# A decode step with sparse attention on one core: fewer transfers for the sample queries and masks, and the last four output tiles in two passes over the tokens

## The reference, cut to what matters

```python
# 512 prompt tokens and 8 x 4 sample tokens, D_MODEL 2048, 8 heads x 128
q, k, v, ga, qi, ki, wi, u, gb = _project(x, pos, w_in)        # one input projection
# attention: an indexer scores all causal keys, each query keeps the best k
scores = _index_scores(qi, wi, ki_all)          # samples: 1024 cached + 4 new keys
_, idx = lax.top_k(scores, topk)
s = einsum(q, k_sel) * HEAD_DIM ** -0.5         # samples read paged keys and values
o = softmax(s) @ v_sel
# pooling mixer p: trailing means over 2/4/8/16 tokens, then a 256 x 256 map per group
mixed = concat([a * silu(ga), p * silu(gb)])
h = DEEPNORM_ALPHA * x + einsum('btc,cd->btd', mixed, w_out)
mu, var = mean(h, -1), mean((h - mu) ** 2, -1)
y = (h - mu) * rsqrt(var + LN_EPS) * ln_g + ln_b
```

## Time and profile before

| what | value |
|---|---|
| median of 3 runs | 1173.95 us (1172.24 to 1175.3) |
| the profiled execution's own time | 1169.77 us |
| its span, first to last instruction | 1168.0 us |
| busy, share of the span | PE 96%, PEld 90%, DVE 54%, ACT 27%, POOL 30% |
| mean granted TensorE clock | 0.985 |
| chain that ended last, by engine | PE 82%, DVE 7%, SP's queue 4%, issue 3%, DMA 3% |

### The profile page before, as it was taken

How to read it: one execution, slowest core, us unless ns; L and a number is a source line. 1 busy time by engine, 2 the same in 40 slices (tenths; PEclk the granted TensorE clock), 3 DMA queues, 4 the chain that set the end, 5 groups by cost and what they waited for, 6 DMA issues and landing times.

```text
span 1168.0 us, 29727 instructions
## 1 busy us (share of the span) xinstructions
PE 1126.3 (96%) x11836; PEld 1048.8 (90%) x11836; DVE 636.5 (54%) x1173; ACT 318.4 (27%) x593; POOL 354.4 (30%) x150
## 2 busy tenths in 40 slices
PE   6999999999999999999997889999999999999995
PEld 5888889999999999999997888888889889999992
DVE  3566667896547557562364574655546443232236
ACT  4333334223332322332231221211212332122111
POOL 2323222333334334333330313221322233443410
PEclk9999999999999999999999999999999999999996
DMA  8542242233333333335414799788878785233103
GB/s 259 135 113 78 64 113 69 80 92 94 83 83 82 83 92 95 88 98 157 118 28 105 245 327 296 259 302 271 302 254 295 231 281 143 73 89 90 54 0 153
DMA packets 202157, 171.56 MB, mean 147 GB/s; under 512 B 22802, under 2 KB 182986, under 8 KB 200818
## 3 DMA queue, kind: packets, MB, share of 16 engines
q1 hardware_dynamic: 188666, 161.40, 44.8%
q10 hardware_dynamic: 13376, 8.53, 2.4%
HBM read 159.57 MB, written 9.90 MB: 145 GB/s over the span
## 4 chain that ended last, share of the span: by engine, by line
PE 82%; DVE 7%; SPq 4%; issue 3%; DMA 3%; ACT 1%; DVEq 0%; ACTq 0%
PE acc L1126 66%; PE acc L1490 2%; PE bank L1184 2%; PE bank L1427 2%; PE acc L1543 2%; PE bank L1301 1%; DVE scoreP L1753 1%; PE bank L1320 1%; DVE top L1749 1%; PE acc L1454 1%; SPq L455 1%; DMA xnat<-in_x_prompt 1%; SPq L561 1%; SPq L458 1%; DVE win L1994 1%
## 5 line engine op out<-in xcount | busy, mean ns | idle before, releaser
L653 POOL TENSOR_TENSOR wL<-rawW,wH 128x1024 fp32r<-128x1024 f32 (+1 forms) x146 | 354.2, 2427 | 766.5 <-ACT wH L675 766.5
L1126 PE MATMUL acc<-actH,wH 128*128 128x272 f32 (+1 forms) x2304 | 493.6, 296 | 1.2 <-DVE actL L1667 1.2
L1126 PE MATMUL acc<-actH,wL 128*128 128x272 f32 (+1 forms) x2304 | 477.6, 289 | 0.0
L1126 PE MATMUL acc<-actL,wH 128*128 128x272 f32 (+1 forms) x2304 | 476.4, 288 | 0.0
L1126 PEld LDWEIGHTS acc<-actH,wH 128*128 128x128 f32 (+1 forms) x2304 | 361.6, 189 | 31.5 <-issue 29.8
L1126 PEld LDWEIGHTS acc<-actL,wH 128*128 128x128 f32 (+1 forms) x2304 | 362.8, 189 | 0.0
L1126 PEld LDWEIGHTS acc<-actH,wL 128*128 128x128 f32 (+1 forms) x2304 | 360.3, 189 | 0.0
L675 ACT ACTIVATE wH<-rawW 128x1024 fp32r<-128x1024 f32 (+1 forms) x146 | 153.2, 1053 | 272.2 <-PE acc L1126 241.2
L2098 DVE SCALAR_TENSOR_TENSOR y<-y,bank 128x512 f32 (+1 forms) x16 | 11.0, 688 | 123.5 <-PE bank L1607 121.5
L1705 DVE SCALAR_TENSOR_TENSOR scoreP<-relu,wiN,scoreP 128x256 f32<-128x256 f32 (+2 forms) x54 | 45.4, 881 | 33.4 <-ACT relu L732 33.4
L1858 DVE STREAM_TRANSPOSE kPage<-kPage 128x1024 f32<-128x1024 f32 x30 | 37.2, 1239 | 46.5 <-DMA kPage<-in_cache_k 45.6
(11 more groups left out here) (210 smaller groups left out, 928.3 us busy)
## 6 DMA issues: line engine op xcount, KB each, us to landing
rawW<-in_w_in SPq DMA_DIRECT2D x112, 512.0 KB, 3.9
vPage<-in_cache_v SPq DMA_DIRECT2D x64, 512.0 KB, 7.0
kPage<-in_cache_k SPq DMA_DIRECT2D x60, 512.0 KB, 5.0
rawW<-in_w_out SPq DMA_DIRECT2D x32, 512.0 KB, 3.9
y<-in_x_prompt SPq DMA_DIRECT2D x4, 1024.0 KB, 8.0
out_y_prompt<-y SPq DMA_DIRECT2D x8, 512.0 KB, 2.8
xnat<-in_x_prompt SPq DMA_DIRECT2D x2, 1024.0 KB, 7.7
xnat<-in_x_prompt ACTq DMA_DIRECT2D x2, 1024.0 KB, 11.3
```

Of the source, the lines that this page charges most:

```text
L653: pool.tensor_tensor(wL[:, slot, :, 0:width], rawW[:, slot, :, 0:width], wH[:, slot, :, 0:width].bitcast(F32), ALU.subtract).then_inc(stag ...
L1126: last = pe.matmul(acc[t.slot][0:width, e, 0:HT], w[:, u.slot, k, 0:width], a[:, kk, e * HT:(e + 1) * HT], start=(half == 0 and k == 0 and ...
```

## The change

Three parts.

- **Queries.** `qS` is stored once to DRAM (`qD`), SP waits for that store, and four transfers, one for each strip of 32 partitions, read it back, instead of 16.
- **Masks.** DVE writes the table straight in the order that the mask wants (`dropS`, in the tile `U`, which is not in use yet), in two `tensor_scalar` and a memset; eight transfers of whole rows store it; and each mask is one transfer whose source is repeated for the four quarters, here and in the groups. ACT and DVE wait for the stores before they write `U`.
- **Output.** The first twelve tiles stay. The last four are multiplied for tokens 0 to 255 first, then their weights are loaded and split again and they are multiplied for tokens 256 to 543 (`out_part`: 24 matmuls with each half of a weight tile). The statistics, shift, correction and last pass of tokens 0 to 255 stand between the late parts.

```diff
+TWICE = 4
+WHOLE = KC - TWICE
+EARLY_T = 2 * P
...
-                for j in range(QUARTERS):
-                    stand_alone(sp)
-                    sp.dma_start(probS[SPAN * j:SPAN * (j + 1), :],
-                                 dropD.rearrange("s a r c -> (s a) r c")[:, ds(at, NT), :]).then_inc(mask_in[x % 2], 16)
+                stand_alone(sp)
+                sp.dma_start(probS[:], dropD.rearrange("b s a t c -> b (s a t) c")[ds(at, 1), :, :]
+                             .to_broadcast([QUARTERS, SPAN, LP])).then_inc(mask_in[x % 2], 16)
...
+            sp.dma_start(qD.rearrange("j s n -> (j s) n"), qS[:].rearrange("p h n -> p (h n)")).then_inc(q_out, 16)
+            sp.wait_ge(q_out, 16)
             for side in range(SIDES):
-                for j in range(SIDES):
-                    sp.dma_start(qAll[STREAK * side:STREAK * (side + 1), j, :],
-                                 qS[STREAK * j:STREAK * (j + 1), :, :].rearrange("p h n -> p (h n)")).then_inc(q_spread, 16)
+                sp.dma_start(qAll[STREAK * side:STREAK * (side + 1), :, :], qD.rearrange("j s n -> s j n")).then_inc(q_spread, 16)
...
             for side in range(SIDES):
                 for a in range(HALF):
-                    sp.dma_start(dropD[side, a, :, 0:HP].rearrange("r (p n) -> r p n", p=PAGES),
-                                 scoreS[:, 0:PAST].rearrange("r (p s n) -> r p s n", p=PAGES, s=SIDES)[:, :, side, :]
-                                 ).then_inc(drop_out, 16)
-            for a in range(HALF):
-                sp.dma_start(dropD[0, a, :, HP:LP], scoreS[:, PAST:L]).then_inc(drop_out, 16)
-            sp.dma_start(dropD[1:SIDES, :, :, HP:LP].rearrange("s a r c -> r (s a) c"),
-                         outside[0:NS, 0:NS].unsqueeze(1).to_broadcast([NS, (SIDES - 1) * HALF, NS])).then_inc(drop_out, 16)
+                    sp.dma_start(dropD[:, side, a, :, :], dropS[:, side, :]).then_inc(drop_out, 16)
...
+            for j in range(TWICE):
+                load_tile(wo_view, (WHOLE + j) * P, TILE_D + KC + j)
...
+            def out_part(tile, half):
+                t, u = tile_turn(tile), turn(2 * tile + half, 4)
+                e, cols = (0, slice(0, EARLY_T)) if tile < TILE_D + KC else (1, slice(EARLY_T, T))
+                pe.wait_ge(stage_ready[u.slot], u.read)
+                if half == 0:
+                    pe.wait_ge(acc_copied[t.slot], t.free)
+                for k in range(HU):
+                    for w, parts in ((wH, (actH, actL)), (wL, (actH,))):
+                        for a in parts:
+                            last = pe.matmul(acc[t.slot][:, e, 0:cols.stop - cols.start], w[:, u.slot, k, :],
+                                             a[:, (1 - half) * HU + k, cols], start=(half == 0 and k == 0 and w is wH and a is actH),
+                                             stop=(half == 1 and k == HU - 1 and w is wL))
+                last.then_inc(tile_ready[t.slot] if half else stage_free[u.slot // 2], 1)
...
+            for n in range(WHOLE + 1, KC + 2):
+                out_part(TILE_D + n, 0)
+                part_rows(n - 1)
+                out_part(TILE_D + n, 1)
             shift_turned("t0", (0, 1), 2)
+            out_part(TILE_D + KC + 2, 0)
+            part_rows(KC + 1)
             pe.wait_ge(gb_in, 16 * 8)
+            shift_back("t0")
+            correction(0, (0, 1))
+            out_part(TILE_D + KC + 2, 1)
+            correction(0, (2, 3))
+            out_part(TILE_D + KC + 3, 0)
+            part_rows(KC + 2)
+            correction(1, (0, 1))
+            out_part(TILE_D + KC + 3, 1)
+            correction(1, (2, 3))
+            part_rows(KC + 3)
             shift_turned("t1", (2, 3, 4), 4)
...
-                    own.step(dve.memset(outside[0:NS, 0:NS], MASKED))
-                    own.wait()
-                    dve.tensor_scalar(scoreS[:], scoreS[:], PICKED / 1.5, MASKED, ALU.is_gt, ALU.mult).then_inc(drop_ready, 1)
+                    dve.memset(dropS[:, 1:SIDES, HP:LP], MASKED)
+                    dve.tensor_scalar(dropS[:, 0, HP:LP], scoreS[:, PAST:L], PICKED / 1.5, MASKED, ALU.is_gt, ALU.mult)
+                    dve.tensor_scalar(dropS[:, :, 0:HP].rearrange("r s (p n) -> r s p n", p=PAGES),
+                                      scoreS[:, 0:PAST].rearrange("r (p s n) -> r p s n", p=PAGES, s=SIDES),
+                                      PICKED / 1.5, MASKED, ALU.is_gt, ALU.mult).then_inc(drop_ready, 1)
```

More of the change, by code:

```diff
@@ L1616, in _, with part_rows @@
                     unit(TILE_D + j + 1, 1, i, 2)
-            unit(TILE_D + KC - 1, 0)
-            rows(0, 7)
-            unit(TILE_D + KC - 1, 1)
-            rows(1, 7)
+            unit(TILE_D + WHOLE - 1, 0)
+            rows(0, 5)
+            unit(TILE_D + WHOLE - 1, 1)
+            def part_rows(n):
+                copied(TILE_D + n)
+                j, late = n % 2, n >= KC
+                b = tb(f"{'ab'[late]}{n - (KC if late else WHOLE)}")
+                dst = take(b)
+                for at in range(2):
+                    t = at + 2 * late
+                    last = pe.transpose(dst[:, at * P:(at + 1) * P], raw[:, j, t * P:(t + 1) * P], ident)
+                if late:
+                    last = pe.transpose(dst[0:NS, 2 * P:3 * P], raw[:, j, NP_:T], ident)
+                full(b, last)
             def shift_turned(name, tiles, ready):
@@ L1641, in _ @@
             pe.wait_ge(gb_in, 16 * 8)
-            b = tb("t0")
-            pe.wait_ge(bank_free[b.slot], b.read)
-            correction(0)
-            shift_turned("t1", (2, 3, 4), 4)
-            b = tb("t1")
-            pe.wait_ge(bank_free[b.slot], b.read)
-            for n in (2, 3):
-                take(tb(f"t{n}"))
-            for t in range(1, TT + 1):
+            shift_back("t0")
+            correction(0, (0, 1))
+            out_part(TILE_D + KC + 2, 1)
+            correction(0, (2, 3))
@@ L2124, in _, with part_added, part_gained @@
                     gained(2 * i + j)
-                own.leave(KC // 2 - 1)
+                own.leave(WHOLE // 2)
             own.step(dve.memset(mv[:], 1.0))
-            for j in range(2):
-                residual(KC - 2 + j, j, KC // 2 - 1)
-                statistics(KC - 2 + j)
-                if j == 0:
-                    gained(KC - 2)
+            def part_added(n):
+                late = n >= KC
+                d = n - TWICE if late else n
+                cols = slice(d * P, (d + 1) * P)
+                lo = 2 * late
+                b = tb(f"{'ab'[late]}{n - (KC if late else WHOLE)}")
+                src = bank_wait(dve, b)
+                if late:
+                    at = y[0:NS, TT, cols]
+                    own.step(dve.scalar_tensor_tensor(at, at, ALPHA, src[0:NS, 2 * P:3 * P], ALU.mult, ALU.add))
+                at = y[:, lo:lo + 2, cols]
+                dve.scalar_tensor_tensor(at, at, ALPHA, src[:, 0:2 * P].rearrange("p (t c) -> p t c", t=2),
+                                         ALU.mult, ALU.add).then_inc(bank_free[b.slot], 1)
+                own.wait()
+                dve.wait_ge(bank_free[b.slot], b.read)
+                for t in range(lo, TT + 1 if late else 2):
+                    m = P if t < TT else NS
+                    own.step(dve.bn_stats(bn[0:m, t, d, :], y[0:m, t, cols]))
+                own.wait()
+            def part_gained(n):
+                late = n >= KC
+                d = n - TWICE if late else n
+                cols = slice(d * P, (d + 1) * P)
+                lo = 2 * late
+                own.step(dve.tensor_tensor(y[:, lo:lo + 2, cols], y[:, lo:lo + 2, cols],
+                                           gbc[:, cols].unsqueeze(1).to_broadcast([P, 2, P]), ALU.mult))
+                if late:
+                    own.step(dve.tensor_tensor(y[0:NS, TT, cols], y[0:NS, TT, cols], gbc[0:NS, cols], ALU.mult))
             def aggregate(tiles):
```

138 lines of the change are left out of this document (97 added, 41 removed).

## The result

The changed kernel takes 1158.89 us (median of 6 runs, 1156.77 to 1160.58), the kernel before 1172.12 us (median of 6, 1167.22 to 1175.30): ratio 0.9886, 95% interval 0.9865 to 0.9906. So it is 13.2 us faster. The forecast was 1162.0 us, in a range from 1155 to 1169, on the right side and 3.1 us too high. Of these 3.1 us, 1.8 are the kernel before, whose median was 1173.95 us in three runs and is 1172.12 us in six; of the gain itself 11.9 us were forecast and 13.2 us came.

What follows compares the result with a forecast made beforehand. Bound: the order in SP's queue at the start of the page transfers, PE itself behind it, and the tail. 9.1 us (queries, masks) + 2.8 us (output) = 11.9 us off 1173.95 gave 1162.0 us, range 1155 to 1169.

Steps and rivals of the forecast that it cites:

- SP passes the first mask 9.9 us earlier: SP's queue ahead of the first mask's end: queries save 3.8 us, table 3.7, the mask's issue 2.4.
- The waits for the mask and the key pages go: PE in the first group: waits of 1.0, 2.2 and 2.4 us vanish, and 1.8 us of half clock.
- The issue stalls: PE's two waits for its own program: 1.7 us (0 to 3.2) off the first, the second left at 2.03 us.
- Sum of part 1 up to the first group's end: Queries and masks together: 1.7 + 1.0 + 2.2 + 1.8 + 2.4 = 9.1 us gained on PE.
- The last of these three counts in the groups too: The shorter mask issue saves about 2.5 us per mask in the groups, counted at nothing because PE is the bound.
- PE's stream in part 2: Output in two passes: 0.5 us of transposes and small matmuls plus 2.9 us for three correction pairs, 3.4 us longer.
- The tail: From the last output part's end to the kernel's end: 19.6 us instead of 25.83, a gain of 6.2 us.
- Rival A: Both issue stalls on PE go and its clock stays up: about 3 us more gained, 1159.0 us; chance 0.13.
- B: PE waits again: first issue stall stays whole, the last key pages' wait returns; 1166.2 us, chance 0.20.
- C: Corrections in the output stage cost 2.1 us a pair: 1165.5 us; chance 0.13.
- D: Query store's wait eats the issues' saving, SP early by masks alone, middle gives 3 us: 1168.2 us; chance 0.05.
- E: POOL cannot feed PE in the last 16 half tiles; at 4.0 us each the kernel is slower, 1178 us; chance 0.03.

Runs made afterwards that it cites:

- `q_only`: The kernel before with only the queries changed (one store, four loads); table, masks and output as before: 1167.99 us against 1171.45 (ratio 0.9970).
- `table_mask`: The kernel before with only the table (eight stores) and masks (one transfer each) changed; queries and output as before: 1163.88 us (ratio 0.9929).

## Why the prediction was right, and where its steps were off

- **SP passes the first mask 9.9 us earlier.** Right: 9.85 us. From the queries' being ready to the next key pages' issue 10.99 us became 7.17, so 3.8 as forecast, with 2.9 us of waiting for exponentials in it; from the table's first store to the mask 10.93 became 7.40, 3.5 for 3.7, the eight whole rows costing 0.72 us each where 0.55 was taken; the mask's issue 3.17 became 0.64, 2.5 for 2.4. In the first of these two errors cancel: the store and the four loads took 3.4 us with SP's wait, not 5.4, and the exponentials 2.9 us, not 1.
- **The waits for the mask and the key pages go, 1.0 + 2.2 + 2.4 us, and the half clock behind one of them, 1.8 us.** Right: no bracket is left on these rows, and the clock from 660 to 680 us is 1.00. The last pages have 1.7 us to spare, not 0.8. That is not much: there is a wait of 2.08 us for them with the masks in four, and one of 1.06 us with 24 empty instructions and the masks unchanged, so not all of the 2.08 us need be the masks'.
- **The issue stalls, 1.7 us off the first, the second as it was.** Half right: 3.23 and 2.03 became 1.85 and 2.58, 0.8 us in all, so two stalls near 2 us are left where the prediction's signs named one. Over the traces the first is 1.4 to 1.9 us wherever the queries go in five transfers, and 2.7 to 3.2 us with 16. Its cause, small table pieces, was misnamed: `q_only` keeps those pieces and has 1.66 us, `table_mask` has whole rows and 2.67 us, with its stores still being issued from 630.98 to 637.38 us, beside the stall. What fits all traces is whether the stores are over by then; no run tests it by itself. The second stall, counted as unchanged, is 2.0 to 3.7 us with five transfers and 1.2 to 3.4 us with 16, and both together 3.6 to 5.3 us against 4.2 to 6.1 us. So even the 0.8 us is no clear gain.
- **Sum of part 1 up to the first group's end, 9.1 us.** Measured 9.5, but not by these terms alone: as measured they give 0.8 + 1.0 + 2.2 + 1.8 + 2.4 = 8.2 us. Outside the sum are a stall of 0.5 us put down to issue (at 688.97 us before, none after) and the clock behind the two issue stalls, 0.57 from 637 to 645 us before and 0.79 after. Over the six traces with the whole of part 1 and this stretch unedited, the gain from the first key product on is 7.4 to 9.5 us.
- **"The last of these three counts in the groups too ... I count it at nothing."** Wrong by 1.9 us. PE had no idle time from 700 to 720 us, but the waits of 1.59 us for a key page and 0.59 us for a value page stood near 760 us, outside the windows that this step rested on. The pause in SP's loop and the old mask's 3.38 us, which no row reaches, stood ahead of them.
- **PE's stream in part 2 3.4 us longer.** Mis-sized: 4.8 us. The pair of corrections was nearly right, 1.06 us for 0.96, and so was the pace of 119 and 133 ns. What wasn't counted is that each break in the row of matmuls costs about 0.1 us ahead of it and 0.1 us behind it. Of the 1.4 us too little, the three pairs are about 0.3 us and the breaks around them about 0.7 us; the rest is the wait of 0.3 us for the shift and the further transposes.
- **The tail 19.6 us.** Right: 19.96. With the stream, part 2 gives 1.0 us in this trace, 1.2 by the runs, where 2.8 was forecast.
- **POOL feeds PE.** Right: 2.39 us each in the last parts, and PE's only wait from the first half part to the last is 0.3 us for the shift.

The two errors, 1.9 us too little and 1.7 us too much, cancel: that the sum is so near is in part luck. The rest of the shifts, 2.6 us lost at the start and 1.7 us gained between 770 and 940 us, where single stalls put down to issue (1.62 and 0.70 us before, 1.15 and 0.80 us after) and the granted clock (0.91 from 800 to 820 us before) differ, I can't assign to the change: such stalls and spells differ from trace to trace, and the stretch from the table's third line to the output projection's first transposes varies from 180.4 to 183.9 us over traces with the same program there.

Rival A fell: both stalls are there. B fell: no page is waited for, and the first stall isn't whole. C fell: 1.06 us a pair. D fell at SP's rows, and E at POOL's.

## What to carry to other kernels

When one queue feeds several engines, add up its issues ahead of the first transfer that somebody waits for: each 1 us taken off there was worth nearly 1 us here, until the waits behind it were used up. Here that lead lasted until the queue waited for the engine that it feeds: in the second group nothing of it was left. Search the whole trace for waits before calling a stage bound by an engine; one clean window says nothing about the next group. Splitting a long row of matmuls has a price for each break, some 0.2 us, which is to be set against the tail that it shortens.

## What was not expected of the hardware

SP stood still for 6 to 7 us at the start of a later round of its loop over the groups (near 725 us, and near 800 us from 800.61 to 806.86 us with the masks in four), with no wait in the profile, and 10 or 11 instruction packets passed where 1 or 2 pass without the pauses. Moving the loop by 24 instructions brings this on. The Trainium skill, "Runtime: NRT & Kernel Launch", section "Instruction fetch mechanics", says that a taken branch to a place outside a window of two pages makes the engine fetch the page before it goes on; the pause, the packets and the effect of the place agree, while q14's packets are some 8 KB (0.09 MB / 11) where the Trainium skill has 16 KiB, which is what PE's have (1.43 MB / 87). That q14 is SP's is inferred from the edits that change its count.

DVE's product of `y` with the gain takes 2.61 us beside POOL's subtraction (2.40 us, from 1091.67 us) and 0.41 us where none runs. The Trainium skill, "SBUF — State Buffer", section "Who interferes with whom", says that a VectorE instruction with two SBUF inputs contends with a GpSimd instruction that reads SBUF, and that the lock is exclusive; the trace agrees. Here it cost nothing, as DVE had 2.3 us to spare in each part.
